# Hybrid encoder layer on one Trainium2 core: most of the modulation and of the normalised input moved out of the first stage

## The reference, cut to what matters

```
ada = silu(c) @ w_ada + b_ada                 # w_ada is 1024 x 6144; c is one row of 1024, one c for each of two groups
sh1, sc1, gt1, sh2, sc2, gt2 = split(ada, 6)
h = rms_norm(x, norm_pre_mix) * (1 + sc1) + sh1
x = x + gt1 * rms_norm(token_mixer(h), norm_post_mix)
h = rms_norm(x, norm_pre_ffn) * (1 + sc2) + sh2
out = x + gt2 * rms_norm(expert_choice_ffn(h), norm_post_ffn)
```

## Time and profile before

| | |
|---|---|
| Median of three runs | 3905.72 us (3895.16 to 3907.7) |
| Profiled execution | 3897.49 us, its span 3895.8 us |
| TensorE busy in the span | 91% |
| VectorE, ScalarE, GpSimd busy | 56%, 41%, 17% |
| Mean granted TensorE clock | 0.951 of full |

### The profile page before, as it was taken

The page is one execution under the profiler, slowest core; times in us unless marked ns, Lnnn a source line. Parts: engine busy times, 40 slices in busy tenths (PEclk is TensorE's granted clock), DMA queues, the critical chain, the costliest instruction groups (busy, mean ns, idle before and its releaser), DMA issues. The chain is left out here.

```text
span 3895.8 us, 56808 instructions
## 1 busy us (share of the span) xinstructions
PE 3536.0 (91%) x21432; PEld 2934.1 (75%) x21432; DVE 2169.3 (56%) x3920; ACT 1593.3 (41%) x2374; POOL 651.0 (17%) x709
## 2 busy tenths in 40 slices
PE   7699999998889999979999928999999999999991
PEld 3377777766667777757878728999999999999991
DVE  1344534554568888745545465565555555555555
ACT  1344545544334344334444303444444444443442
POOL 0010100101023443402322200011110001000005
PEclk9799999999999999989999858999999999999996
DMA  9733432421754554456555434555555555555567
GB/s 303 238 120 87 136 115 86 130 86 64 232 169 137 168 155 138 120 168 204 187 185 187 154 135 157 157 167 169 170 174 161 165 164 175 172 162 166 162 218 272
DMA packets 544843, 634.46 MB, mean 163 GB/s; under 512 B 77560, under 2 KB 431896, under 8 KB 543776
## 3 DMA queue, kind: packets, MB, share of 16 engines
q1 hardware_dynamic: 506960, 493.72, 40.4%
q0 software_dynamic: 35840, 123.75, 10.0%
q10 hardware_dynamic: 1872, 14.68, 0.9%
HBM read 505.20 MB, written 126.88 MB: 162 GB/s over the span
## 5 line engine op out<-in xcount | busy, mean ns | idle before, releaser
L2414 DVE TENSOR_TENSOR moe_w_lo<-moe_w_raw,moe_w_hi 128x2048 fp32r<-128x2048 f32 x192 | 439.9, 2291 | 371.5 <-ACT moe_w_hi L2362 338.5
L103 PE MATMUL moe_pg<-moe_x_hi,moe_w_hi 128*128 128x320 f32 x2048 | 635.5, 310 | 1.4 <-DVE moe_x_lo L2452 1.4
L104 PE MATMUL moe_pg<-moe_x_lo,moe_w_hi 128*128 128x320 f32 x2048 | 633.8, 309 | 0.0
L105 PE MATMUL moe_pg<-moe_x_hi,moe_w_lo 128*128 128x320 f32 x2048 | 633.8, 309 | 0.0
L2362 ACT CAST moe_w_hi<-moe_w_raw 128x2048 fp32r<-128x2048 f32 x192 | 364.9, 1900 | 158.2 <-DMA moe_w_raw<-in_w_gate_e_dram 81.2
L103 PEld LDWEIGHTS moe_pg<-moe_x_hi,moe_w_hi 128*128 128x128 f32 x2048 | 385.3, 188 | 2.4 <-issue 1.5
L104 PEld LDWEIGHTS moe_pg<-moe_x_lo,moe_w_hi 128*128 128x128 f32 x2048 | 385.4, 188 | 0.6
L105 PEld LDWEIGHTS moe_pg<-moe_x_hi,moe_w_lo 128*128 128x128 f32 x2048 | 385.3, 188 | 0.0
L103 PE MATMUL gla_pd<-gla_h_hi,gla_w_hi 128*128 128x512 f32 x640 | 261.1, 408 | 34.5 <-DVE gla_h_lo L1012 31.9
L103 PE MATMUL pa_pu<-pa_h_hi,pa_w_hi 128*128 128x512 f32 (+1 forms) x560 | 226.9, 405 | 37.4 <-DVE pa_h_lo L644 37.4
L105 PE MATMUL gla_pd<-gla_h_hi,gla_w_lo 128*128 128x512 f32 x640 | 252.4, 394 | 0.0
(11 more groups left out here) (326 smaller groups left out, 7664.0 us busy)
## 6 DMA issues: line engine op xcount, KB each, us to landing
moe_w_raw<-in_w_gate_e_dram SPq DMA_DIRECT2D x64, 1024.0 KB
moe_w_raw<-in_w_up_e_dram SPq DMA_DIRECT2D x64, 1024.0 KB
moe_w_raw<-in_w_down_e_dram SPq DMA_DIRECT2D x64, 1024.0 KB
gla_w_raw<-in_w_in_dram SPq DMA_DIRECT2D x80, 512.0 KB, 4.0
pa_w_raw<-in_w_in_dram SPq DMA_DIRECT2D x35, 1024.0 KB
front_w<-in_w_ada_dram SPq DMA_DIRECT2D x24, 1024.0 KB, 11.9
scratch_gate<-gla_sg POOLq DMA_DIRECT2D x80, 256.0 KB, 2.3
mix_sg<-scratch_gate SPq DMA_DIRECT2D x40, 512.0 KB, 4.6
```

The lines of the kernel that those rows point to most:

```text
L103: pe.matmul(out, w_hi, x_hi, start=start, stop=False)
L104: pe.matmul(out, w_hi, x_lo, start=False, stop=False)
L105: return pe.matmul(out, w_lo, x_hi, start=False, stop=stop)
L2414: dve.tensor_tensor(w_lo[:, m % 2], w_raw[:, m % 2], w_hi[:, m % 2].bitcast(F32), ALU.subtract).then_inc(s_wlo, 1)
```

## The change

`phase_front` now loads 8 chunks of `w_ada` (sh1 and sc1) and makes `K.a1`, `K.b1` and h of block 0 alone. All chunks have a buffer of their own. A chunk's 8 products go to four groups of 32 partitions (k % 4), and the four partial rows are summed by the product that turns rows to columns. `silu(c)` is kept in `K.cS`.

`phase_proj_attn` makes h of block b + 1 in block b, one tile of 128 tokens at a time, in the places of four tables: `SQUARES` (ACT, after units 1, 4, 7, 10), `NORMS` (DVE, after 2, 5, 9, 13), `TURNS` (PE, after 3, 6, 11, 15), `EVICTS` (ACT and DVE, after 4, 7, 12, 16). A tile's 8 transposes are two "units" of four with a bank each in the ring of three. POOL makes the reciprocal root and stores the tile to DRAM. In the last block 16 chunks of `w_ada` are loaded by POOL into the same buffer `x`, one after each of the first 16 dense units (`ADA`); each is 8 products on four partition groups, an ACT copy, and four small stores.

`phase_mix` loads the 8 partial rows and `b_ada`, makes `K.a2`, `K.b2` at m = 1 and 2 (`ada_columns`), and both gates at m = 3 to 6 (`spread_gate`, 8 products, `gates` on DVE); gate2 goes to DRAM. `router_bias` moves from m = 2, 4 to m = 4, 5.

```diff
+TURNS = {3: 0, 6: 1, 11: 2, 15: 3}
+SQUARES = {1: 0, 4: 1, 7: 2, 10: 3}
+NORMS = {2: 0, 5: 1, 9: 2, 13: 3}
+EVICTS = {4: 0, 7: 1, 12: 2, 16: 3}
+ADA = {j: n for n, j in enumerate([j for j, u in enumerate(BLOCK_UNITS) if u[0] != "la"][:N_ADA])}
...
+        for j in range(NU):
+            order.append(("unit", b, j))
+            if b < NB - 1 and j in TURNS:
+                order += [("turn", b * TPB + TURNS[j], 0), ("turn", b * TPB + TURNS[j], 1)]
+            if b == NB - 1 and j in ADA:
+                order.append(("ada", ADA[j], 0))
...
# SP, phase_proj_attn
+                    if b < NB - 1:
+                        load_x(4 * b)
+                        load_x(4 * b + 1)
                     for c in range(3, NCH + 2):
                         if c < NCH or b < NB - 1:
                             load_w(b * NCH + c)
-                        if c == 7 and b < NB - 1:
+                        if c in (7, 8) and b < NB - 1:
+                            load_x(4 * b + c - 5)
+                        if c == 9 and b < NB - 1:
                             for k in range(RING):
                                 load_h(4 * (b + 1) + k)
...
# ACT
+                def squares(i):
+                    act.wait_ge(s_x[i % 2], 16 * (i // 2 + 1))
+                    wait(act, s_rstd, i)
+                    for n in range(2):
+                        wait(act, s_sq, 2 * i + n)
+                        act.activation(junk, x[:, i % 2, n * D // 2:(n + 1) * D // 2], ACT.Square,
+                                       accum_out=ss[:, n:n + 1]).then_inc(s_sq, 1)
+                def first_half(i):
+                    n = UNIT_NO["turn", i, 0]
+                    act.wait_ge(s_unit, n + 2)
+                    for k in range(KD // 2):
+                        ins = act.activation(x[:, i % 2, k * P:(k + 1) * P], pu[n % BANKS][:, k * P:(k + 1) * P], ACT.Identity,
+                                             bias=K.b1[:, 1, k:k + 1], scale=K.a1[:, 1, k:k + 1])
+                    ins.then_inc(s_ha, 1)
...
                         if kind == "gv" and i == 0:
                             act.wait_ge(s_exp, b + 1)
                             act.activation(soft[:], soft[:], ACT.Ln, bias=1.0).then_inc(s_ln, 1)
+                        if b < NB - 1 and j in EVICTS:
+                            first_half(b * TPB + EVICTS[j])
+                        if b < NB - 1 and j in SQUARES:
+                            squares(b * TPB + SQUARES[j])
+                        if b == NB - 1 and j in ADA:
+                            read_ada(ADA[j])
...
# POOL
+                def load_ada(i):
+                    if i >= N_ADA:
+                        return
...
+                        pool.wait_ge(s_unit, UNIT_NO["ada", i - 1, 0] + 1)
+                    for n in range(2):
+                        pool.dma_start(x[:, n].rearrange("p (k n) -> p k n", n=CW),
+                                       ada[:, 4 * n:4 * n + 4, i * CW:(i + 1) * CW]).then_inc(s_ada[n], 16)
...
# PE
-                    b, j = (n - BANKS) // NU, (n - BANKS) % NU
+                    what, b, j = ORDER[n - BANKS]
+                    if what == "turn":
+                        pe.wait_ge(s_hd if j else s_ha, b + 1)
+                        return
...
+                def ada_rows(i):
+                    n = UNIT_NO["ada", i, 0]
+                    bank_free(n)
+                    for k in range(KD):
+                        if k % 4 == 0:
+                            pe.wait_ge(s_ada[k // 4], 16 * (i + 1))
+                        ins = pe.matmul(pu[n % BANKS][k % 4 * 32:k % 4 * 32 + 2, 0:CW], K.cS[:, k, :],
+                                        x[:, k // 4, k % 4 * CW:(k % 4 + 1) * CW], start=k < 4, stop=k >= 4)
+                    ins.then_inc(s_unit, 1)
```

More of the change, by code:

```diff
@@ L156, in phase_front @@
[L156 to L167, removed]
+        hT = M.sb("hT", [P, KD, BLK])
+        pa = [M.ps(f"pa{i}", [P, 2 * CW]) for i in range(NCH // 2)]
+        pc = M.ps("pc", [P, 2, KD, 2])
+        pt = [M.ps(f"pt{i}", [P, BLK]) for i in range(3)]
+        bank = [pt[0], pt[1], pt[2], pa[0], pa[1], pa[2], pa[3], pt[0]]
+        s_c, s_small, s_x = M.sem("c_loaded"), M.sem("small_loaded"), M.sem("x_loaded")
@@ L183, in _ @@
[L183 to L196, removed]
@@ new lines, in _ @@
+                act.wait_ge(s_c, 32)
+                act.activation(sig[:], cT[:], ACT.Sigmoid).then_inc(s_sig, 1)
+                pair(0)
+                act.wait_ge(s_x, 16)
+                for t in range(TPB):
+                    ins = act.activation(junk[:, t], x[:, t], ACT.Square, accum_out=ss[:, t:t + 1])
+                ins.then_inc(s_sq, 1)
+                for m in range(1, NCH // 2):
+                    pair(m)
+                act.wait_ge(s_mod, 1)
+                for k in range(0, KD, 2):
+                    act.wait_ge(s_t, k + 1)
+                    act.activation(hT[:, k], bank[k][:], ACT.Identity, bias=K.b1[:, 0, k:k + 1],
+                                   scale=K.a1[:, 0, k:k + 1]).then_inc(s_ha, 1)
@@ L255, in chunk, with columns @@
                     mm.then_inc(s_chunk, 1)
[L257 to L262, removed]
-                    ins.then_inc(s_col, 1)
[L265 to L269, removed]
-                        wait(pe, s_out, r if r <= 4 else r - 1)
-                        pe.matmul(gate_bank(r), pick[:, g], row[:, GATES[n], h * 512:h * 512 + 512],
-                                  start=True, stop=True).then_inc(s_row, 1)
+                def columns(j):
+                    pe.wait_ge(s_row, 2 * j + 2)
+                    for k in range(KD):
+                        ins = pe.matmul(pc[:, j, k, :], row[:, 2 * j + k // 4, k % 4 * P:k % 4 * P + P], pick[:],
+                                        start=True, stop=True)
+                    ins.then_inc(s_col, 1)
@@ L274, in _, with turn @@
+                def turn(k):
+                    if 3 <= k < 7:
+                        pe.wait_ge(s_row, k - 2)
+                    if k == 7:
+                        pe.wait_ge(s_ha, 1)
+                    for t in range(TPB):
+                        ins = pe.transpose(bank[k][:, t * P:(t + 1) * P], x[:, t, k * P:(k + 1) * P], K.ident[:])
+                    ins.then_inc(s_t, 1)
                 pe.wait_ge(s_silu, 1)
+                for n in range(NCH - 2):
+                    chunk(n)
@@ L297, in _ @@
-                spread(1)
+                pe.wait_ge(s_xn, 1)
+                for k in range(3):
+                    turn(k)
+                chunk(NCH - 2)
+                chunk(NCH - 1)
+                pe.wait_ge(s_eye, 1)
+                columns(0)
+                columns(1)
+                for k in range(3, KD):
+                    turn(k)
             @block.vector
             def _(dve):
-                step = [0]
-                def link(ins):
-                    step[0] += 1
-                    ins.then_inc(s_v, 1)
-                    dve.wait_ge(s_v, step[0])
```

392 lines of the change are left out of this document (249 added, 143 removed).

## The result

| | before | after |
|---|---|---|
| Median of four runs | 3900.44 us | 3996.43 us (3978.89 to 4006.46) |
| Ratio | 1 | 1.0239, 95% interval 1.0205 to 1.0274 |
| Span of the profiled execution | 3895.8 us | 3991.9 us |

A forecast was written before the change was run, and what follows sets the result against it. TensorE was taken to bound the projections, transfers the first stage. First stage -119.5, turns +14, ring +73.6, clock +12, ada +23, mixer +13.5 sum to +16.6 us: 3918 forecast, range 3868 to 3956.

The forecast's parts named there:

- First stage: Front: fewer weights and less x to load, next stage starts at about 49.5 instead of 169.0, -119.5 us.
- Turns and chunks of ada: Projections: transposes of 16 tiles, +14 us; 16 chunks of ada in the last block, +23 us.
- that rival: Last block: column groups don't run side by side, 3.7 us a chunk of ada, 42 more, 3960; chance 0.10.
- 5 us of waits: Last block: share of the +23 us for ada, allowed for chunks not there in time.
- rival "chunks late": Last block: ada loads wait behind POOL's result stores, 2 us more for each of 16, 32 more, 3950; chance 0.12.
- the prediction's side estimate: Last block: half a chunk of ada transfers in 3.2 us, so no chunk late and the sum 5 lower.
- Ring of banks: Projections: TensorE waits for evictions or late x at units 5, 8, 12, 13 and 17, +73.6 us.
- the upper case of the forecast: Projections: the four evictions of `first_half` take 1.5 us, if each costs all of the 128x256 form.
- The rival in which stalls overlap: Projections: ACT and DVE work ahead while TensorE stands, so next waits are shorter; 49 less, 3869; chance 0.22.
- The clock: Projections: half speed behind long TensorE stops, +12 us; zero if the clock holds, 24 if the others count too.
- eight of these: Projections: the waits at units 17 and 12 in four blocks, each with 3.4 us of half speed, about 1.5 lost.
- The mixer: Start of the mixer: spreading products, two sets of columns and waits, +13.5 us; 8 if waits fall into existing stops.

The follow-up runs named there:

- e3: Changed kernel with turned tiles evicted right behind their step and x of the fourth tile loaded ahead of weight chunk 8: 3874.94 us, ratio 0.9927.
- e5: e3 with unit v moved behind the first unit of q: 3874.22 us, ratio 0.9925.
- e7: e3 with unit v behind the first unit of q and ada from unit 2 on: 3873.27 us, ratio 0.9922.
- e8: The kernel before with unit v behind the first unit of q: 3926.36 us, ratio 1.0050.
- e9: e3 with ada from unit 2 on and a block's first two x loads held until the fourth part of h landed: 3840.40 us, ratio 0.9835.

## Why the prediction was wrong

- **First stage.** Right: 49.9 against 49.5.
- **Turns and chunks of ada.** Right. Eight transposes span 1.04 us, a chunk's 16 records 1.04; four column groups do run side by side, so that rival is out: 3.7 us a chunk on one group by 1.04 is 3.6 times as fast. The Trainium skill, "TensorE: Matmul & The Clock Gate", Part 3, has 2.38 for three column tiles; the trace agrees in kind and is better than the 1.6 us that I had worked out from it. "5 us of waits" measured 9.3, in two chunks. The first comes 6.5 us late in two parts (5.9 and 0.6), the fifth 2.8 (2.15 and 0.7), and both loads stood in POOL's order behind a store of results: the first behind that of block 3's last unit, the fifth, 2.7 us after its buffer was free, behind one of the attention output, for which POOL had waited 8.3 us. The fifth also took 6.7 us to land where the one before it took 4.3. All half chunks landed 3.9 to 7.3 us from issue, 5.2 in the median, where the prediction's side estimate had 3.2. So the mechanism of the rival "chunks late" is real, but in 2 chunks of 16 and not in all, so that its 32 us are out.
- **Ring of banks.** Right place by place: 28.1 at unit 17 (27 forecast), 10.4 at unit 5 (9.8), 13.1 at unit 8 (11.2), 19.7 at unit 12 (17.6), 8.7 at unit 13 (8). The four evictions of `first_half` took 1.50 us (single ones 0.45, overlapping), which is the upper case of the forecast and not the 1.2 that I chose; unit 12 was 2.1 dearer for the late x. The rival in which stalls overlap did not happen: each stop came at full length. The ring's stops and what hangs on them are worth some 3% of the time (ratio 0.9927 for e3, 1.0239 for the changed kernel).
- **The clock: this step failed.** The mechanism was right, a stop and half speed behind it, but the term was mis-sized. The forecast let "eight of these" stops cost 1.5 us each and counted the rest at nothing. In the ten traces every stop over 2.5 us but one was followed by a dip, and six in ten of those of 1.7 to 2.5 us. In the changed kernel 16 short dips cost 1.7 to 4.0 us each, 2.6 in the mean, so the term is 42 us instead of 12. Its upper bound, 24, was too low as well, since it took one price from the one stop of 7 us in the trace of before.
- **What was not in the sum at all:** three dips of some 24 to 31 us over unit v, 37.8 us. One follows the 5.9 us wait for the first chunk of ada. Two follow stops that were there before and that grew from 1.4 to 1.6 us to 1.8, because x is loaded behind the part of h for which the unit waits. The growth makes a dip likelier, by the count above, and not certain: block 3's stop of 1.92 us had none, and whether one comes and lasts differs from execution to execution. I had listed the loads of x as part of unit 12's stall, and not asked what they do to the transfer in front of them.
- **The mixer.** Right, 12.6 against 13.5.

Of the 78.6 us that the projections came out dearer than forecast, 69 are thus lost work (30 in the short dips, 38 in the long ones, 1 at the start), 6.4 the ring, 4.3 the waits for ada and 2 other standing, less 3 in turns and chunks. Taken together, stage by stage: -119.1 + 201.2 + 12.6 + 2.6 - 1.2 = 96.1, the difference of the two spans.

## What to carry to other kernels

Price a stop of TensorE with the dip behind it: here 2 us of standing cost up to 2 more, and 5 to 7 us cost 1.5 to 3 more. Then ask what the engine runs next: the unit of 96 products of 128 columns, where it began in a dip, ran at half speed to its end in 16 of 23 cases, 12 to 14 us each. Work on a busy engine can be moved there at little more than its own price if its inputs and its buffers are ready early: the same move of work that lost 2.4% gains 1.65% with the eviction one unit earlier and the loads of x and ada re-placed. And look up in the order of the issuing engine what a late load stands behind before you name the buffer it waits for.

## What was not expected of the hardware

- Of the stops of 1.7 to 2.5 us in these ten traces 21 of 35 were followed by a granted clock of 0.50, of the shorter ones from 1.2 us on 4 of 72, of the longer ones 47 of 48. Behind short stops the fall comes when work has begun again (104.5 to 106.6 stood, low from 107.0 to 110.4); in the 7 us stop it came within it.
- At the low clock unit v takes 20.2 us instead of 10.4 with TensorE busy without a gap, and the clock rises 2.3 to 6.4 us after the unit's end, when 512-column products run. In units of 512 or 256 columns it rose 2.8 to 7.5 us after the end of the last stop, in block 0 of e5, e7 and e8 after 9.2 to 9.5. In the eight dips over v behind short stops (up to 2.2 us) the five long ones had fallen 0.4 to 1.4 us before v began, the three that ended within v 1.7 to 1.9 us before. No run changed the shape of v's products, so that it is their 128 columns which keep the clock low is argued from these rows and not shown; nor do the runs show why dips behind like stops come in some executions only (in after, 1.83 us with a long one, 1.92 with none).
- Two 512 KB loads queued 0.4 us behind another of 512 KB on the same queue delay its landing: 4.15 to 4.69 us from issue in nine cases, against 3.75 to 4.12 in fifteen without them. The wait for it grows by as much (1.85 us in the changed kernel, 1.43 in e9, both in block 1).
